# Norms of a two-layer streaming trunk: where the low parts of the rows are computed, the order of the first two weight tiles, and how the last square is summed

## The reference

```python
rmsnorm(x, g) = x * rsqrt(mean(x*x) + 1e-6) * g
layer 0: x += lru_mixer(rmsnorm(x));   x += conv_ffn(rmsnorm(x))
layer 1: x += rwkv7_mixer(rmsnorm(x)); x += conv_ffn(rmsnorm(x))
y = rmsnorm(x)
conv_ffn(h): u = causal_dwconv(h @ w_up); g, val = split(u); (gelu(g) * val) @ w_down
```

## Time and profile before

| | us |
|---|---|
| median of 3 runs | 3357.98 (3354.85 to 3358.43) |
| profiled execution, its time | 3362.65 |
| profiled execution, span | 3360.9 |
| TensorE busy in the span | 3054.0 (91%) |
| VectorE, ScalarE, GpSimd busy | 1665.3, 1156.7, 969.2 |
| mean granted TensorE clock | 0.969 |

### The profile page before, as it was taken

One profiled execution on the slowest core, in us unless ns is written; L12 is line 12 of the kernel. 1 busy time (PEld: TensorE's weight loads), 2 busy tenths in 40 slices (PEclk: granted clock), 3 DMA queues, 4 the chain that ended last, 5 costly groups with the idle time before them and its releaser, 6 DMA issues.

```text
span 3360.9 us, 73562 instructions
## 1 busy us (share of the span) xinstructions
PE 3054.0 (91%) x32214; PEld 2948.5 (88%) x32214; DVE 1665.3 (50%) x1691; ACT 1156.7 (34%) x1334; POOL 969.2 (29%) x521
## 2 busy tenths in 40 slices
PE   5999799999999998699968888886979999999996
PEld 5899689999999997699967777775979999999996
DVE  6555655454445456102206767774364444544445
ACT  4634332221222224434325666665132222212222
POOL 2222222222222224213313333434122222222221
PEclk9999899999999998799979999998989999999998
DMA  2111111111111110332222212212101111111111
GB/s 99 43 33 42 32 33 45 45 45 45 44 45 45 45 45 26 128 135 85 84 93 56 68 55 64 68 45 83 45 32 45 45 45 44 41 50 44 45 45 60
DMA packets 87562, 186.10 MB, mean 55 GB/s; under 512 B 28896, under 2 KB 51936, under 8 KB 87264
## 3 DMA queue, kind: packets, MB, share of 16 engines
q1 hardware_dynamic: 80352, 154.73, 14.7%
q10 hardware_dynamic: 6912, 26.84, 2.0%
HBM read 145.01 MB, written 36.53 MB: 54 GB/s over the span
## 4 chain that ended last, share of the span: by engine, by line
PE 79%; DVE 11%; ACT 4%; issue 2%; POOL 2%; DMA 1%; ACTq 0%; SPq 0%; DVEq 0%; POOLq 0%
PE PS L1110 68%; PE PS L1270 11%; DVE T L1545 2%; ACT T L461 2%; DVE T L1535 1%; DVE G L1535 1%; POOL HL L902 1%; DVE HL L1535 1%; DVE M L1550 1%; DVE X L1535 1%; DVE NN L1535 1%; PE PS L1223 1%; ACT L461 1%; PE PS L1142 1%; DVE HF L1545 1%
## 5 line engine op out<-in xcount | busy, mean ns | idle before, releaser
L902 POOL TENSOR_TENSOR WL<-RAW,WH 128x1024 fp32r<-128x1024 f32 x204 | 499.0, 2446 | 1512.7 <-ACT WH L461 1508.8
L1110 PE MATMUL PS<-HH,WH 128*128 128x364 f32 x3456 | 774.2, 332 | 77.8 <-POOL HL L902 43.1
L1110 PE MATMUL PS<-HH,WL 128*128 128x364 f32 x3456 | 770.5, 331 | 0.0
L1110 PE MATMUL PS<-HL,WH 128*128 128x364 f32 x3456 | 768.3, 331 | 0.0
L1110 PEld LDWEIGHTS PS<-HH,WH 128*128 128x128 f32 x3456 | 603.6, 190 | 91.3 <-issue 46.5
L1110 PEld LDWEIGHTS PS<-HH,WL 128*128 128x128 f32 x3456 | 608.6, 190 | 0.0
L1110 PEld LDWEIGHTS PS<-HL,WH 128*128 128x128 f32 x3456 | 606.9, 190 | 0.0
L1535 DVE TENSOR_TENSOR X<-PS,X 128x1092 f32<-128x1092 f32 x224 | 290.3, 1296 | 279.5 <-PE PS L1110 275.0
L1545 DVE SCALAR_TENSOR_TENSOR T<-T,FP 128x1092 f32<-128x1092 f32 x192 | 415.9, 2166 | 6.8
L461 ACT ACTIVATE WH<-RAW 128x1024 fp32r<-128x1024 f32 x204 | 216.5, 1061 | 367.3 <-PE PS L1110 344.7
L461 ACT ACTIVATE T<-PS 128x1092 f32<-128x1092 f32 (+1 forms) x125 | 135.5, 1084 | 601.2 <-PE PS L1110 580.7
(11 more groups left out here) (156 smaller groups left out, 3434.4 us busy)
## 6 DMA issues: line engine op xcount, KB each, us to landing
RAW<-weights SPq DMA_DIRECT2D x204, 512.0 KB, 3.6
scratch<-T ACTq DMA_DIRECT2D x32, 546.0 KB, 2.9
scratch<-SR ACTq DMA_DIRECT2D x16, 546.0 KB, 2.9
X<-xT SPq DMA_DIRECT2D x8, 546.0 KB, 8.2
yT<-T SPq DMA_DIRECT2D x8, 546.0 KB, 3.0
T<-scratch_m SPq DMA_DIRECT2D x8, 512.0 KB, 4.1
LW<-scratch SPq DMA_DIRECT2D x16, 192.0 KB, 2.6
KK<-scratch SPq DMA_DIRECT2D x16, 192.0 KB, 3.2
```

Of the source, the lines that this page charges most:

```text
L902: pool.tensor_tensor(out, full, hi, ALU.subtract).then_inc(*t.made(event))
L1110: mm = pe.matmul(acc[:, j, :], a, b[:, j * CW:(j + 1) * CW], start=(i == 0 and q == 0), stop=(i == len(blocks) - 1 and q == 2))
```

## The change

Six things, of which the diff shows the core:

- In the three stages and in the projections' HS rows, DVE alone makes the low parts of the rows after a norm: row 0, row 1, low 0, row 2, low 1, and so on. POOL no longer has these 16 instructions. The rows that follow later in the projections, and those that the output product loads back, keep their alternation.
- The first two tiles of a stage are computed together (`up_two`): for each k both tiles, each WH·HH, WL·HH, then WH·HL. PE waits for `h_hi` at the start of k, and for the low part only before the third product of the first tile.
- The projections' paired tiles put the four products with HS first and the two with HSL last, with the same two waits.
- In a norm DVE makes 6 additions. PE multiplies the sum of seven squares by ones, and then the last square (T[:, 5]) by ones into the same accumulator: twice as many matmuls.
- ACT takes Ln of one column right after the last square, before the weights' high parts that follow ("primed"), so the first table load stands there.
- The end rows go to eight rows of HF, and no row waits for a transfer.

The counts that SP and ACT wait for are changed to match (`lows`).

```diff
+ALONE = 3 * KT
+
+
+def lows(name, rows):
+
+    both = (rows - ALONE) // 2
+    return both + ALONE if name == "h_lo1" else both
...
-                sp.dma_start(io["yT"][k], T[:, 4 + k % 2, 0:COLS]).then_inc(*t.made(f"dma_y{k % 2}"))
+                sp.dma_start(io["yT"][k], HF[:, k, PAD:ROW]).then_inc(*t.made(f"dma_y{k % 2}"))
...
-                        act.wait_ge(*t.at("summed", t.n.get("squared", 0) // KT * (KT - 1) + k - 2))
+                        act.wait_ge(*t.at("summed", t.n.get("squared", 0) // KT * (KT - 2) + k - 2))
                     run(T[:, 3 if k == 0 else 4 + k % 2, 0:COLS], X[:, k, :], ACT.Square, "squared")
+                run(DV[:, 13, 0:1], CO[:, 0:1], ACT.Ln, "primed")
                 if weights == "both":
...
-            for k in range(KT):
-                h_lo(k)
+            t.n["h_hi"] = KT
...
-            for k in range(KT):
-                h_lo(k)
+            t.n["h_hi"] += KT
             ffn()
...
-            for k in range(KT):
-                if k % 2:
-                    t.n["h_hi"] += 1
-                else:
-                    rest(HSL[:, k, :], HF[:, k, PAD - 2:ROW], HS[:, k, :], "h_hi", "h_lo")
+            t.n["h_hi"] += KT
...
-            for k in range(KT):
-                h_lo(k)
             ffn()
...
+            def up_two(m, n, row):
+
+                for q in range(2):
+                    pe.wait_ge(*t.next("w_lo"))
+                    if m + q >= 2:
+                        pe.wait_ge(*t.at(f"taken{(m + q) % 2}", (m + q) // 2))
+                for k in range(KT):
+                    pe.wait_ge(*t.at("h_hi", row + k + 1))
+                    for q in range(2):
+                        w, acc = (n + q) % 2, ACC[(m + q) % 2]
+                        for i, (a, b) in enumerate(((WH[w], HH), (WL[w], HH), (WH[w], HL))):
+                            if q == 0 and i == 2:
+                                pe.wait_ge(*t.next("h_lo1"))
+                            for j in range(CH):
+                                mm = pe.matmul(acc[:, j, :], a[:, k, :], b[:, k, j * CW:(j + 1) * CW],
+                                               start=(k == 0 and i == 0), stop=(k == KT - 1 and i == 2))
+                        if k == KT - 1:
+                            mm.then_inc(*t.made("acc_ready"))
...
             def norm(m):
 
-                pe.wait_ge(*t.next("summed", KT - 1))
                 if m >= 2:
                     pe.wait_ge(*t.at(f"taken{m % 2}", m // 2))
+                pe.wait_ge(*t.next("summed", KT - 2))
                 for j in range(CH):
-                    mm = pe.matmul(ACC[m % 2][:, j, :], ONES, T[:, 3, j * CW:(j + 1) * CW], start=True, stop=True)
+                    pe.matmul(ACC[m % 2][:, j, :], ONES, T[:, 3, j * CW:(j + 1) * CW], start=True, stop=False)
+                pe.wait_ge(*t.next("squared", KT))
+                for j in range(CH):
+                    mm = pe.matmul(ACC[m % 2][:, j, :], ONES, T[:, 5, j * CW:(j + 1) * CW], start=False, stop=True)
                 mm.then_inc(*t.made("acc_ready"))
...
-                for q in range(3):
-                    up(m + q, n + q, fresh=(g == 0 and q == 0))
+                if g == 0:
+                    up_two(m, n, 0)
+                for q in range(2 if g == 0 else 0, 3):
+                    up(m + q, n + q)
                 gates(m + 3, 2 * g)
...
-                    for q in range(4):
-                        up(m + q, n + q, fresh=fresh and q == 0)
+                    if fresh:
+                        up_two(m, n, row)
+                    for q in range(2 if fresh else 0, 4):
+                        up(m + q, n + q)
                     return m + 4, n + 4
...
-                pe.wait_ge(*t.next("h_lo1" if k % 2 else "h_lo"))
+                pe.wait_ge(*t.at("h_hi", 2 * KT + k + 1))
                 for q in range(2):
                     acc = ACC[(m + q) % 2]
                     s, sh, sl = (n + q) % 2, TR[:, 6 + q, k * P:(k + 1) * P], TR[:, q, k * P:(k + 1) * P]
-                    for i, (w, x, c) in enumerate(((WH[s][:, k, :], HS, 2), (WH[s][:, k, :], HSL, 2), (WL[s][:, k, :], HS, 2),
-                                                   (sh, HS, 1), (sh, HSL, 1), (sl, HS, 1))):
+                    for i, (w, x, c) in enumerate(((WH[s][:, k, :], HS, 2), (WL[s][:, k, :], HS, 2), (sh, HS, 1), (sl, HS, 1),
+                                                   (WH[s][:, k, :], HSL, 2), (sh, HSL, 1))):
+                        if q == 0 and i == 4:
+                            pe.wait_ge(*t.next("h_lo1"))
                         for j in range(CH):
...
-            def h_rows(name, at, event="h_full"):
+            def h_rows(name, at):
 
                 dve.wait_ge(*t.next("rstd"))
                 for k in range(KT):
-                    if event == "hf":
-                        out = HF[:, k, PAD:ROW]
-                    elif name == "final":
-                        out = T[:, 4 + k % 2, 0:COLS]
-                        if k >= 2:
-                            dve.wait_ge(*t.at(f"dma_y{k % 2}", k // 2))
-                    else:
-                        out = T[:, 4 + k % 4, 0:COLS]
-                        if k >= 4 and k % 2 == 0:
-                            dve.wait_ge(*t.at("h_lo", (at + k - 4) // 2 + 1))
-                    stt(out, X[:, k, :], vec(name, k), T[:, 2, 0:COLS], ALU.mult, ALU.mult, event)
-                    if event == "h_full" and name != "final" and k % 2 == 0 and k:
+                    stt(T[:, 4 + k % 4, 0:COLS], X[:, k, :], vec(name, k), T[:, 2, 0:COLS], ALU.mult, ALU.mult, "h_full")
+                    if k:
                         h_lo(at + k - 1)
-                if event == "h_full" and name != "final":
-                    h_lo(at + KT - 1)
+                h_lo(at + KT - 1)
...
                 if last:
-                    add_squares(KT - 1)
+                    t.n["squared"] += 1
...
-                if k and k % 2 == 0:
+                if k:
                     rest_of(k - 1)
...
-            h_rows("final", 0)
+            dve.wait_ge(*t.next("rstd"))
+            for k in range(KT):
+                stt(HF[:, k, PAD:ROW], X[:, k, :], vec("final", k), T[:, 2, 0:COLS], ALU.mult, ALU.mult, "h_full")
```

More of the change, by code:

```diff
@@ L249, in build @@
             dma_y0 dma_y1 dma_st
-            w_hi w_lo acc_ready taken0 taken1 pads vprep absv hist kept tap conv gelu squared summed rstd
+            w_hi w_lo acc_ready taken0 taken1 pads vprep absv hist kept tap conv gelu squared primed summed rstd
             h_full h_hi h_lo h_lo1 h_used mixhalf hf p_full p_hi p_lo tan root post
@@ L371, in _ @@
             sp.wait_ge(*t.at("acc_ready", M_OUT))
-            sp.wait_ge(*t.at("h_lo", 6 * KT // 2))
-            sp.wait_ge(*t.at("h_lo1", 6 * KT // 2))
+            for name in ("h_lo", "h_lo1"):
+                sp.wait_ge(*t.at(name, lows(name, 6 * KT)))
             weight(W_OUT)
@@ L435, in _ @@
             for k in range(4, KT):
-                sp.wait_ge(*t.at("h_lo1" if k % 2 else "h_lo", 6 * KT // 2 + k // 2 - 1))
+                name = "h_lo1" if k % 2 else "h_lo"
+                sp.wait_ge(*t.at(name, lows(name, 6 * KT) + k // 2 - 1))
                 if k == KT - 1:
@@ L625, in mix_half @@
                     j, k = MIXES[halves // KT], halves % KT
-                    before = (3 * KT + halves - k) // 2
                     name = "h_lo1" if k % 2 else "h_lo"
+                    before = lows(name, 3 * KT + halves - k)
                     if halves < KT:
@@ L632, in mix_half @@
                     elif k == 0:
-                        act.wait_ge(*t.at("h_lo", before))
-                        act.wait_ge(*t.at("h_lo1", before))
+                        for name in ("h_lo", "h_lo1"):
+                            act.wait_ge(*t.at(name, lows(name, 3 * KT + halves)))
                     elif k >= 6:
@@ L667, in _ @@
             w_hi(n + 1, m + 2)
-            act.wait_ge(*t.at("h_lo", 3 * KT // 2 + 3))
-            act.wait_ge(*t.at("h_lo1", 3 * KT // 2 + 3))
+            for name in ("h_lo", "h_lo1"):
+                act.wait_ge(*t.at(name, lows(name, 3 * KT) + 3))
             run(TR[:, 2, 0:COLS], lora_g, ACT.Copy, "lora_hi")
@@ L1173, in _, with ffn @@
             m += 1
-            def ffn(m, n):
+            def ffn(m, n, row):
                 def step(m, n, fresh=False):
-                    for q in range(4):
-                        up(m + q, n + q, fresh=fresh and q == 0)
+                    if fresh:
+                        up_two(m, n, row)
+                    for q in range(2 if fresh else 0, 4):
+                        up(m + q, n + q)
                     return m + 4, n + 4
@@ L1187, in ffn @@
                 return down(m, n, STEPS - 1)
-            m, n = ffn(m, n)
+            m, n = ffn(m, n, KT)
             norm(m)
@@ L1522, in _ @@
             m += 1
-            m, n = ffn(m, n)
+            m, n = ffn(m, n, 7 * KT)
             norm(m)
@@ L1634, in _ @@
```

(3 more changed lines are left out.)

## The result

The changed kernel takes **3326.76 us** (median of 4 runs, 3324.22 to 3332.39), the kernel before 3357.69 beside it. The ratio is 0.9906, 95% interval 0.9894 to 0.9919: 31 us gained, where 20.3 were forecast, and the time lies 0.24 us under the forecast's range. The profiled execution has a span of 3324.1 us and took 3325.93, against 3360.9 and 3362.65, so the traces' spans differ by 36.8 us.

What follows compares the result with a forecast made beforehand. TensorE's matmuls bound the kernel, busy 3054 of 3360.9 us. Stages 18.3 + projections 2.3 + end 5.2 - norms 5.5 = 20.3 us, taken from the median 3357.98: 3337.7; own range 3332 to 3343, 8 in 10 3327 to 3347.

Steps and rivals of the forecast that it cites:

- Paired stages: LRU and both FFNs: paired first tiles and VectorE's low parts end the third tile earlier, 5.2, 6.5 and 6.6 us.
- the clock's two prices: Paired stages: lower clock costs 2.3 us at the pair's start (bounds 0, 2.8) and 3.0 in the third tile.
- rival A: Clock doesn't fall in the 3.3 us wait before the third tile, giving back 9 us: 3328.7 us; chance 0.13.
- The race at WL: After the first tile, GpSimd's subtraction starts 0.24 us ahead of VectorE's tap; otherwise 4 us less gain.
- Low parts by VectorE: Three stages: with GpSimd idle, a row takes VectorE 1.39 us and a low part 1.30, staying ahead of TensorE.
- rival D: VectorE, making all the low parts, doesn't keep up in the three stages: 3382 us, slower than before; chance 0.04.
- C: VectorE's and ScalarE's chain sets the step; stages bring 5.3 us, not 18.3: 3350.7 us; chance 0.09 with E.
- E: Pairing brings nothing, as the fourth tile waits for what the third no longer covers; near C; chance 0.09 with C.
- Projections: Paired tiles there: the start no longer waits for GpSimd's first low part, gaining 2.3 us (bounds 0 and 2.8).
- Norms: Five norms: one addition fewer but twelve matmuls instead of six, 1.1 us lost each, 5.5 in all.
- B: Norms stay at the lower clock throughout (5.8 us more) and the tap gets ahead of GpSimd: 3345.5 us; chance 0.14.
- End: Last eight rows no longer wait for transfers: 5.2 us gained, bounds 3 and 5.5.

Runs made afterwards that it cites:

- experiment 1: Kernel before with 72 already satisfied waits (36 instructions) added at TensorE's start, nothing else changed: 3349.64 us, ratio 0.9969.
- experiment 7: Changed kernel with the norm of before (seven additions, one group of matmuls) and 72 waits at TensorE's start: 3323.38 us, ratio 0.9892; five kernels have that norm.
- experiment 11: Kernel before with only the first two tiles of the three stages paired, low parts still by GpSimd and VectorE in turn: 3341.87 us, ratio 0.9954.
- experiment 8: Changed kernel without the primed Ln after each norm's last square: 3324.28 us, ratio 0.9905.
- experiment 2: Changed kernel with 440 satisfied waits (220 instructions) at TensorE's start, taking the shift back modulo 256: 3343.17 us, ratio 0.9944.
- the kernel with 24 places: Changed kernel with the norm of before and 24 extra wait instructions on TensorE behind the first norm: 3321.90 us, ratio 0.9887.

## Why the prediction was wrong

The mechanisms that it named were all there. What failed is a step it didn't write: it took the sections that the edits leave alone at nothing, and gave no reason.

- **Failed: the sections without edits, taken as 0.** The chunk section gave 11.8 us of the 36.8 between the traces. Between the medians 10.6 us were gained beyond the forecast, and the shift alone gave 10.5 (6.7 to 13.8) in experiment 1. The prediction counted the twelve matmuls of a norm by their time only, and not that 36 more instructions displace the 35,000 of the chunk section. Nor did the waits that it read from the page include the section's issue waits, 29.2 us in 51, a larger entry than VectorE's low parts.
- **Paired stages, 18.3 forecast, 21.5 in the trace: mechanism right, the clock's two prices too high in two of three stages.** First matmul at R + 2.64 (2.55 forecast), no wait inside the pair, WL wait 3.6, 3.33 and 3.4 (3.3). But the pair's start at the lower clock cost 1.6 in LRU and the first FFN (the 135 matmuls to the first tile's end took 24.1 instead of 22.5), and 2.5 in the second FFN, where 2.3 was taken; and the third tile took 13.84 twice and 14.94 once, not 15.0. In the first FFN's 4.79 us with the wait the mean clock is still 1.00, in the tile 0.88: the level fell after TensorE had begun again, and rose before the tile's end. In the earlier trace rows it had already fallen in the wait. So in the changed kernel the clock fell each time, and rival A is two fifths true in two stages and not at all in the third. But it is no law of the wait: in the first FFN of experiment 7's kernel the same wait was followed by a tile wholly at the upper level.
- **The race at WL: right.** GpSimd started at 434.26, VectorE's tap at 434.51, and the tap took 3.31. The trace agrees once more with the Trainium skill (SBUF — State Buffer, Who interferes with whom): the one that came first was not held up, 2.40 us against the 2.46 of the earlier trace rows.
- **Low parts by VectorE: right in time, wrong in weight.** Rows at 1.38 and low parts at 1.30, so rival D was off, and the fourth tile followed the third without a wait (12.04 us). From the first FFN's R to the projections' R it takes 8.3 us less (889.0 against 897.3), all that was won at its start, so C and E fell. But the prediction gave one sum for the two edits, and experiment 11 shows that the pair alone brings 7.8 of 8.4.
- **Projections 2.3: 2.4.** First matmul at R + 2.84, pair 50.35 us against 50.80 in the earlier trace rows, WL wait 3.2, the tile 14.8 (15.0).
- **Norms -5.5: -3.9 in the trace**, and 1.5 more in a stage behind them, if experiment 7's five kernels are the measure. The prediction's own working gives 0.9 and not 1.1 for a norm (400.25 + 5.1 + 1.15 = 406.5, against 405.59). In the second norm the first group began at the upper clock and the twelve took 5.6 us, in the last 6.97, all but at the lower level; from the last matmul to R the middle three lost 0.2 to 0.3, the last 2.1 and the first 1.1. So B is wrong for the middle ones and nearly right for the last. What decides the level there stays open, and the idle time alone doesn't: TensorE had idled 3.8 us ahead of the second norm's group, which began at the upper level, and 2.9 ahead of the last norm's, which didn't; in experiment 8 it had idled the same 2.9 ahead of the last norm, and the twelve took 5.6 us at a mean clock of 0.70.
- **End 5.2: 5.8**, alone 4.7 (1.7 to 7.7). **Primed Ln 0: 0.**

Between the medians the edited parts bring about 20 us (31 less the shift's 10.5), which is the forecast. Some of that is luck: in the trace they bring 25.7, with 3.2 more than forecast in the stages, 1.6 in the norms and 0.6 at the end, and one execution of each kernel can't say which is nearer.

The range was too narrow for the same reason as the forecast: its ends were made of the edits' own bounds, and held nothing for a section of 590 us that they only displace.

## What to carry over

Before you cost an edit of a long unrolled stream of short instructions, look for waits with no releaser and count whether they stand a fixed number of instructions apart; if so, any instruction added or removed ahead moves them, here by 10 to 12 us, and every comparison of two versions needs the same shift on both, or several shifts. Of two edits that remove the same wait, test each alone: here either takes most of the gain. And a norm or other small step that gains by more passes on an idle TensorE has to pay for them at whatever clock it finds.

## What the runs showed of the hardware

- TensorE's instructions come in while the program runs. The page of each kernel has a queue of instruction packets (packets, MB, share of 16 engines), here the changed kernel and then the one with 220 more instructions, which needed one packet more:

```profile
q8 instruction: 254, 4.16, 0.5%
```

```profile
q8 instruction: 255, 4.18, 0.5%
```

- A packet of this queue is 16,384 bytes. The trace has 65,196 instructions of TensorE in the changed kernel, 254.7 times 256, so the counts fit a packet of 256 instructions of 64 bytes. One takes 1.10 us in the section before and 0.98 after (medians).
- Of the section's 136 places, one to a block of about 4.3 us, 50 take over 0.4 us before and 34 after. These stalls end at a nearly fixed time after their packet: half of them 1.30 to 1.45 us after its end in the kernel before, and the packet had started 1.5 to 2.0 us before the stall began. At three in four of the places under 0.15 us it had started 2.4 us or more before. Packets and blocks go together in one fixed numbering: in every one of the 14 traces and at each of the 136 places, TensorE went on no sooner than 1.14 us after the end of the packet that belongs to the block. Outside the section, as in the FFNs, where 256 instructions take some 20 us, no such time is over 0.31 us in the kernels before and after and in experiments 1 and 2. What starts a packet's transfer stays open, and with it a way to choose a good place other than by trying. That "a block arrives late" is the cause is read from these times and from the shifts; no run makes the packets themselves faster.
- A wait that is already satisfied is not free: two of them make an instruction, and TensorE takes 108 ns for each such instruction (36 from 5.62 to 9.41 us in experiment 1, 220 from 5.56 to 29.35 in experiment 2). Where the engine is idle for longer anyway, as in experiment 1, that costs nothing. The first norm started 1.0 us later there (22.06 instead of 21.10) because VectorE's additions had begun later. The expectation of the kernel with 24 places takes this 1 us for the waits' cost, which it is not.
- The section differs by several microseconds between executions of kernels that have it at the same place (573.9 to 581.5 at 36, 584.2 to 591.2 at 0), so single traces can't rank versions closer than that.
